# Preparing weights on GpSimd at other points of a 12-step matmul pipeline, and the order of one quarter of the gate products

## The reference, cut to what matters

```python
n   = rmsnorm(h)
z   = n @ W_in                      # q, k, v, gates, and the conv group's cc, cu, gc, cb
y_gla  = gated linear attention of q, k, v
y_conv = cb * causal_conv3(cc * cu) * silu(gc)
h   = h + concat([y_gla, y_conv]) @ W_out
gate = sigmoid(h @ W_ple_gate + b_gate)
h   = h + gate * (p @ W_ple)
out = rmsnorm(h)
```

## Time and profile before

| what | value |
|---|---|
| median of three runs | 2048.13 us (2047.91 to 2050.92) |
| the profiled execution | 2050.24 us, of which the span of the trace is 2048.4 us |
| PE busy | 1983.6 us, 97% of the span |
| DVE, ACT, POOL busy | 1338.9, 782.3, 689.5 us |
| longest chain | 87% of the span on PE |
| PE's waits between 660 and 2030 us | 20.1 us once, 3.2 us once, 0.4 us seven times |

### The profile page before, as it was taken

The page is one execution under the profiler, slowest core; times in us unless marked ns, Lnnn a source line. Parts: engine busy times, 40 slices in busy tenths (PEclk is TensorE's granted clock), DMA queues, the critical chain, the costliest instruction groups (busy, mean ns, idle before and its releaser), DMA issues.

```text
span 2048.4 us, 28892 instructions
## 1 busy us (share of the span) xinstructions
PE 1983.6 (97%) x11266; PEld 1722.9 (84%) x11266; DVE 1338.9 (65%) x1569; ACT 782.3 (38%) x1219; POOL 689.5 (34%) x758
## 2 busy tenths in 40 slices
PE   6999999999999879999999999999999999999996
PEld 4888888888888758888888888888788999999996
DVE  4775667666654365775775775685674577777776
ACT  4354354444433323323333233223223255445543
POOL 3766666666551131231331331255551000000000
PEclk9999999999999989999999999999999999999998
DMA  6345354354446232136532137585587812222222
GB/s 228 136 161 194 135 192 179 144 200 165 161 176 279 96 108 85 67 108 249 183 110 83 60 111 259 198 297 200 191 287 285 321 58 88 93 81 86 83 83 83
DMA packets 88305, 322.84 MB, mean 158 GB/s; under 512 B 11600, under 2 KB 22272, under 8 KB 77184
## 3 DMA queue, kind: packets, MB, share of 16 engines
q1 hardware_dynamic: 55328, 185.46, 24.6%
q0 software_dynamic: 32864, 135.85, 18.3%
HBM read 193.34 MB, written 127.93 MB: 157 GB/s over the span
## 4 chain that ended last, share of the span: by engine, by line
PE 87%; DVE 5%; issue 3%; ACT 2%; DMA 1%; POOL 0%; SPq 0%; DVEq 0%; ACTq 0%; POOLq 0%
PE bank L1220 14%; PE bank L1226 14%; PE bank L1222 14%; PE bank L966 8%; PE bank L974 8%; PE bank L967 8%; PE bank L1312 5%; PE bank L1306 5%; PE bank L1308 5%; PE bank L1053 1%; PE bank L1355 1%; PE bank L1354 1%; PE bank L1353 1%; PE bank L1113 1%; PE bank L1104 1%
## 5 line engine op out<-in xcount | busy, mean ns | idle before, releaser
L1220 PE MATMUL bank<-XH,WC 128*128 128x512 f32 x1344 | 526.2, 392 | 23.4 <-DVE ccs L2031 20.1
L1222 PE MATMUL bank<-XH,WC 128*128 128x512 f32 x1344 | 524.0, 390 | 0.0
L1226 PE MATMUL bank<-XL,WC 128*128 128x512 f32 x1344 | 523.9, 390 | 0.0
L2005 DVE TENSOR_TENSOR XL<-RQ,XH 128x1024 fp32r<-128x1024 f32 x168 | 220.9, 1349 | 244.6 <-ACT XH L1598 243.6
L1220 PEld LDWEIGHTS bank<-XH,WC 128*128 128x128 f32 x1344 | 253.1, 188 | 76.9 <-issue 20.8
L1226 PEld LDWEIGHTS bank<-XL,WC 128*128 128x128 f32 x1344 | 253.0, 188 | 52.7
L1222 PEld LDWEIGHTS bank<-XH,WC 128*128 128x128 f32 x1344 | 253.2, 188 | 52.0
L1312 PE MATMUL bank<-XLg,WC 128*128 128x256 f32 x896 | 254.2, 284 | 2.8 <-DVE XLg L2243 2.8
L1306 PE MATMUL bank<-XHg,WC 128*128 128x256 f32 x896 | 253.5, 283 | 0.0
L1308 PE MATMUL bank<-XHg,WC 128*128 128x256 f32 x896 | 253.4, 283 | 0.0
L1598 ACT ACTIVATE XH<-RQ 128x1024 fp32r<-128x1024 f32 x168 | 170.7, 1053 | 194.4 <-PE bank L1226 148.1
(11 more groups left out here) (216 smaller groups left out, 3651.4 us busy)
## 6 DMA issues: line engine op xcount, KB each, us to landing
WC<-w_scratch SPq DMA_DIRECT2D x28, 2048.0 KB, 8.8
RQ<-n_scratch POOLq DMA_DIRECT2D x32, 1024.0 KB, 5.4
w_scratch<-prep_hi POOLq DMA_DIRECT2D x84, 256.0 KB, 2.3
w_scratch<-PB POOLq DMA_DIRECT2D x84, 256.0 KB, 2.3
n_scratch<-raw SPq DMA_DIRECT2D x8, 2048.0 KB, 7.1
y_scratch<-y_sb SPq DMA_DIRECT2D x64, 256.0 KB, 2.8
RQ<-y_scratch POOLq DMA_DIRECT2D x16, 1024.0 KB, 5.7
xt<-xb_dram SPq DMA_DIRECT2D x64, 256.0 KB, 5.2
```

Source lines behind the costliest of these rows:

```text
L1220: nc.tensor.matmul(bank[:], WC[:, i, q, 0, k], xh, start=(k == 0 and i in (P1, P2, P5)), stop=False, skip_group_check=True)
L1222: nc.tensor.matmul(bank[:], WC[:, i, q, 1, k], xh, start=False, stop=False, skip_group_check=True)
L1226: mm = nc.tensor.matmul(bank[:], WC[:, i, q, 0, k], xl, start=False, stop=(k == 3), skip_group_check=True)
L2005: nc.vector.tensor_tensor(XL[:, k], RQ[:, OPERAND[s % 7], 2 * h:2 * h + 2], XH[:, k].bitcast(F32), ALU.subtract).then_inc(sx_lo, 1)
```

## The change

It has three parts. The strips are spread over steps 1 to 7 (`STRIPS_OF`: none in step 0, four each in steps 1 to 3, three each in 4 to 7) in place of three in each of steps 0 to 7. The units of gate weights are moved: step 9 has none in slot 2, step 10 has five, one and one, and the last two (n = 18 and 19) stand in slot 0 of step 11, ahead of the W_ple tiles; SP's wait for the prepared weights is cut in two to match (the weights of P1, P6, P7 and P2 don't wait for the last two units, P5 does). And in each gate product the first quarter does the low-data matmuls of all four k behind the eight high-data ones.

```diff
-GATE_SLOTS = {NB: (1, 1, 1), NB + 1: (5, 3, 1), NB + 2: (5, 2, 1)}
+STRIPS_OF = (0, 4, 4, 4, 3, 3, 3, 3)
+GATE_SLOTS = {NB: (1, 1, 1), NB + 1: (5, 3, 0), NB + 2: (5, 1, 1), NB + 3: (2,)}
...
                 if i == P1:
-                    wait_prepared(sp, g // NP + 2)
-                    if g == STEPS - 1:
+                    if g < STEPS - 1:
+                        wait_prepared(sp, g // NP + 2)
+                    else:
                         sp.wait_ge(tile_stored, 16 * 2 * STRIPS)
+                        sp.wait_ge(prep_stored[2], 16 * (24 + 8))
+                        sp.wait_ge(prep_stored[5], 16 * (84 + 14))
+                if i == P5 and g == STEPS - 1:
+                    wait_prepared(sp, 4)
                 load_weights(g // NP + 1, i)
...
                 if is_conv(g):
-                    for n in range(3 * g, 3 * g + 3):
+                    for n in range(sum(STRIPS_OF[:g]), sum(STRIPS_OF[:g + 1])):
                         strip(n)
-                elif g in GATE_SLOTS:
+                else:
                     gate_parts(g, 0)
-                elif g == STEPS - 1:
+                if g == STEPS - 1:
                     for n in range(PLE_K):
                         prep_tile(n)
...
-                        xh, xl = XHg[:, z % 2, k], XLg[:, z % 2, k]
+                        xh = XHg[:, z % 2, k]
...
-                        if q == 0 and k == 0:
-                            pe.wait_ge(gx_lo, z + 1)
-                        mm = nc.tensor.matmul(acc_ap, WC[:, i, q, 0, k], xl, start=False, stop=(k == 3),
-                                              skip_group_check=True)
+                        if q > 0:
+                            mm = nc.tensor.matmul(acc_ap, WC[:, i, q, 0, k], XLg[:, z % 2, k], start=False, stop=(k == 3),
+                                                  skip_group_check=True)
+                    if q == 0:
+                        pe.wait_ge(gx_lo, z + 1)
+                        for k in range(4):
+                            mm = nc.tensor.matmul(acc_ap, WC[:, i, q, 0, k], XLg[:, z % 2, k], start=False, stop=(k == 3),
+                                                  skip_group_check=True)
                     mm.then_inc(g_prod, 1)
```

## The result

The changed kernel takes 2024.92 us (median of four runs, 2023.86 to 2026.83), the kernel before 2048.58 us in four runs beside it. The ratio is 0.9884, 95% interval 0.9866 to 0.9901: 23.7 us faster, where the forecast of 2019 meant 29.4. It is inside the range of 2014.5 to 2025.5, but 0.6 us from its upper end, and it is the time of rival (b), which had a chance of 0.2.

The account below looks back on a forecast made before the run. PE, busy 97% of the span, bounds the kernel, so gains are its waits or clock. Terms -21.6 - 4.8 - 4.5 + 1.5 = -29.4 us give 2019 us, range 2014.5 to 2025.5.

Parts of the forecast that it names:

- (b): Step 11 to gate: late xt tiles, PE waits at P3 and first gate product; 5 to 9 us; chance 0.2.
- (a): Whole kernel: all three waits gone, last step costing 0 to 4 us; 2015.5 to 2021 us; chance 0.64.
- last step: Step 11: units ahead of the W_ple tiles delay p_raw, gate weights and XLg; cost 1.5 us, bounds 0 and 9.
- its own sign: A PE wait over 2 us between step 0's P5 and the gate would make the prediction wrong.
- step 0: P5 of step 0: PE's 20.07 us wait and 1.5 us of slow clock go; gain 21.6 us.
- seam 9/10: Seam of steps 9 and 10: PE's 3.2 us wait and 1.55 us of slow clock go; gain 4.8 us.
- gate blocks: Head of P6 in seven gate blocks: the 0.65 us lost waiting for XLg goes; gain 4.5 us.
- Strips in steps 1 to 3: One more strip each, about 7 us, covered by POOL's idle time before t1, 11 us left; cost 0.
- two thirds are caught up in the gaps of the queue by 1600: Step 11's transfer queue: of 4.7 MB moved past 1565, two thirds recovered, leaving about 4 us of delay.
- (c): Step 0: stall only shortened, as heads, t1 and P5's split crowd together; 2025 us; chance 0.07.
- (d): Gate blocks or seam 9/10 give nothing; 4.5 or 4.8 us less gain, 2023.5 us; chance 0.07.
- (e): Change doesn't do what it says at one place, held true of SP's split wait; counted in (a).

Follow-up runs that it names:

- strips_only: Kernel before with only the strips spread over steps 1 to 7; 2027.4 us, ratio 0.9891.
- units_only: Kernel before with only the gate-weight units moved and SP's wait cut in two; 2052.97 us, ratio 1.0017.
- order_only: Kernel before with only the first quarter's low-data matmuls put behind the eight high-data ones; 2044.56 us, ratio 0.9981.
- after: The changed kernel, all three parts of the change against the kernel before; 2024.92 us, ratio 0.9884.
- burst_only: Changed kernel with last two units in step 10 and SP holding P1, P6, P7 gate weights to leave together; 2027.72 us, ratio 0.9898.
- units_back: Changed kernel with units and SP's wait as in the kernel before; 2023.11 us, ratio 0.9867.
- one_strip: Changed kernel with one strip left in step 0 and three instead of four in step 3; 2031.3 us, ratio 0.9918.
- full_wait: Changed kernel with SP's wait for the prepared weights whole again; 2026.5 us in a single run.
- after_again: The changed kernel measured again with no edit; 2025.24 us, ratio 0.9880.
- p_raw_behind: Changed kernel with the p_raw load behind the gate weights of P1, P6 and P7 in SP's queue; 2025.32 us, ratio 0.9874.
- units_in_10_p: Changed kernel with last two units in step 10 and p_raw behind the gate weights of P1, P6, P7; 2018.68 us, ratio 0.9866.
- units_in_10_b: Changed kernel with the last two units in step 10 instead of step 11, second job; 2017.77 us, ratio 0.9857.

## Why the prediction was right, and by how much it was off

The direction, the three gains and the place of the cost were right; one term of the sum had the wrong size. The likeliest case, (a), did not come: it had the last step at 0 to 4 us. The time is in the range because that was drawn wide enough for most of (b), which is luck as far as the last step goes. By its own sign the prediction failed there: it said that a wait of PE of over 2 us between step 0's P5 and the gate would make it wrong, and PE waits 3.50 us, at the place it named as likeliest; and the clock, said to stay at 1.00, falls.

| term | forecast | measured | from |
|---|---|---|---|
| step 0 | -21.6 | -20.1 | steps of strips_only |
| seam 9/10 | -4.8 | -4.7 | units_only, with its 1.6 us at the gate's start set apart |
| gate blocks | -4.5 | -3.9 | gate phase of order_only |
| last step | +1.5 | +6.8 | rows of after at the gate's head; burst_only has 7.6 |
| sum | -29.4 | -21.9 | steps and gate of after: -24.2 |

The measured terms come from single profiles, and their sum is 2.3 us apart from the whole. Some 1.5 of that is the seam of strips_only, where the lower clock happened to last longer; with it step 0 is -21.6 and the sum -23.4. The seam's own price differs as much: PE's wait and the lower clock behind it cost 4.8 us in the kernel before, 6.3 in strips_only, 5.4 in units_back and 2.4 in order_only, where the clock didn't fall. The last step is the only term that is off by more than this, by 5.3 us, and the forecast missed the median by 5.9.

**Step 0.** That POOL's queue and not the data of t1 ended the wait is shown by one_strip, where a single strip brings a wait back and PE again follows t1's start by 7.7 us. The forecast allowed the heads' last operations on DVE to be held up beside t1 by at most 4.64 us. DVE in the changed kernel:

```profile
694.02 0.74 DVE L1888 SCALAR_TENSOR_TENSOR y_sb<-bank,vec,rt 128x512 f32<-128x512 f32 x1
694.80 2.42 DVE L1893 TENSOR_TENSOR y_sb<-y_sb,sg 128x512 f32<-128x512 f32 x1
697.14 0.74 DVE L1888 SCALAR_TENSOR_TENSOR y_sb<-bank,vec,rt 128x512 f32<-128x512 f32 x1
697.92 2.11 DVE L1893 TENSOR_TENSOR y_sb<-y_sb,sg 128x512 f32<-128x512 f32 x1
```

The two with both inputs in SBUF take 2.42 and 2.11 us while t1 runs, 0.69 elsewhere (at 671.53); the two that read a bank keep their 0.74. So t1 costs them 3.2 us, inside the 5.8 of slack. The Trainium skill, SBUF — State Buffer, "Who interferes with whom", says just this of the two kinds of operation, and the rows agree.

**Strips in steps 1 to 3.** Free, as told: POOL still idles 10.4 us in front of each t1 there (forecast 11).

**Seam.** Right. DVE's adds of copies at the seam fall from 10.78 to 6.96 us. In step 10 they take 4.99 (forecast 4.75) and 6.97, and PE doesn't wait.

**Gate blocks.** Right, 0.6 us too high.

**The last step.** Three things were wrong in it, in the order of the working. To compare, I count from the end of step 11's matmuls, 1579.4 here and 1608.4 before. First, the tiles start 16.6 us later by that measure, but take 22.3 us in place of 28.7 (1507.59 to the last store's issue at 1529.94); so `p_raw` goes out 47.1 us ahead in place of 57.3, 10.2 later and not 12 to 16, and t1 isn't late. That was in the forecast's favour, and yet the cost was higher. Second, the step that failed is "two thirds are caught up in the gaps of the queue by 1600, which leaves about 4 us of delay". Windows of 10 us over the last 40 us of the steps show that there are next to no gaps. Before the change (the second, left out, reads 0.96 and 363 GB/s):

```profile
1568.40:1578.40 10.00, 10.00 (x46) 8.29 (x45) 4.35 (x8) 3.48 (x6) 0.00 (x0) 1.00 0.88 322
...
1588.40:1598.40 10.00, 10.00 (x45) 8.26 (x44) 2.59 (x4) 0.62 (x1) 0.00 (x0) 1.00 1.01 404
1598.40:1608.40 10.00, 10.00 (x46) 8.27 (x45) 8.47 (x11) 1.51 (x2) 0.00 (x0) 1.00 0.91 307
```

And after it, all four:

```profile
1539.40:1549.40 10.00, 10.00 (x46) 8.29 (x45) 6.36 (x11) 3.64 (x7) 0.00 (x0) 1.00 1.03 410
1549.40:1559.40 10.00, 10.00 (x46) 8.29 (x45) 8.05 (x11) 2.97 (x3) 0.00 (x0) 1.00 0.89 281
1559.40:1569.40 10.00, 10.00 (x46) 8.29 (x45) 2.69 (x4) 0.00 (x0) 0.00 (x0) 1.00 1.01 419
1569.40:1579.40 10.00, 10.00 (x45) 8.07 (x44) 1.80 (x3) 1.06 (x1) 0.00 (x0) 1.00 0.96 357
```

The share of busy DMA engines is 0.88 to 1.03 in all eight. In the 20 us ahead of them the changed kernel moves 4.1 MB (120 and 290 GB/s), the kernel before 6.0 (308 and 290): 1.9 MB are missing, and ten microseconds before the end of the steps still 1.7. So a tenth and not two thirds was caught up. At some 0.36 MB per us 1.7 MB are 4.7 us (an estimate). What the `xt` is late beyond that I put down to the second burst, which goes out right ahead of it; no run parts the two. Against the end of the steps the `xt` that DVE waits for is issued 1.1 us later and takes 6.1 us longer (17.2 for 11.1), 7.2 together, where I had 4. Two rows of DVE (against the earlier trace rows):

```profile
1577.04 0.69 DVE L2169 TENSOR_TENSOR xt<-xt,EB 128x512 f32<-128x512 f32 x1 [14.95 <-DMA xt<-xb_dram]
...
1583.69 1.22 DVE L2253 TENSOR_TENSOR XLg<-raw,XHg 128x1024 fp32r<-128x1024 f32 x1
```

XLg is done at 1584.91, 7.1 us later against PE than before. PE had 2.6 us of slack for it (1.6, and 1.0 by the new order), which leaves 4.5, and 0.87 and 3.66 were measured. Third, I priced that wait without the slow clock that I had counted behind the two waits of the earlier trace rows; it is 2.3 us here.

On the rate of transfers the Trainium skill, SBUF — State Buffer, "A bandwidth-pool intuition that's wrong", with its usual 358 GB/s, comes closer than my 410: the four windows after the change have a mean of 367 GB/s, those before 349, though single ones reach 419. My 410 was a peak, and a queue that has to be emptied goes by the mean.

**Of the rivals**, (b) is what happened, with its place at the gate's first product right. Its wait at P3 of step 11 didn't come: DVE waits 1.38 us there for an `xt`, at 1554.27, and PE doesn't. (c) and (d) are excluded by strips_only, order_only and units_only. That SP's split wait does nothing, part of (e), fits full_wait, to within 1 us.

## What to carry to other kernels

A transfer queue may wait for side work, as SP here waits for POOL's tiles. Side work moved ahead of that wait is paid for by what stands behind it in the queue. Write down all that follows there until PE's next first use, and look at the share of busy DMA engines over that stretch: at 0.88 to 1.03 the queue here caught up a tenth in 30 us. Large loads that leave together can delay small stores on which the queue's own next wait depends, and then one burst makes the next. And a part of a change can be worth nothing while the whole is 1.2% faster; here the same units one step earlier gave 5 us more.

## What was not expected of the hardware

- The wait of 3.50 us of PE is followed by 4.8 us at half clock, which adds two thirds to its price, and this addition differs from profile to profile: behind the same wait it is 3.1 us at half clock in full_wait, 5.3 in after_again and 6.1 in one_strip. The shortest wait with a fall behind it is 2.88 us (p_raw_behind, granted clock 0.50 from 1553.7 to 1557.1); none follows 2.39 (order_only) and 1.81 us (units_in_10_p). The gap of 0.87 us just ahead of it left the clock at 1.00 (window 1580.28 to 1581.20).
- A 256 KB load of `xt` on SP's queue behind the first three weights lands after 5.0 us where these are spread (units_in_10_b) and after 9.8 where they leave together (the changed kernel); behind the second group it is 12.2 and 17.2.
- The two W_ple tiles take 22.3 us where they start later in step 11 and 28.7 before, with the same instructions: their waits for transfers shrink from 5.3 to 5.7 us each to 2.8 to 4.3. I had taken their time as fixed.
